# Spectra by even and odd tokens, the last modulation group in two parts, and a new order of the first stage

## What is computed

```python
mod = (cond @ w_ada[l] + b_ada[l])[:, None, :]
sh1, sc1, g1, sh2, sc2, g2 = jnp.split(mod, N_MOD, axis=-1)
h = x * (1.0 + sc1) + sh1
z = h @ w_in[l] + b_in[l]
...
k = jnp.concatenate([h_fwd.at[0].add(h_bwd[0]), jnp.zeros((1, ch), h_fwd.dtype), h_bwd[:0:-1]], axis=0)
return jnp.fft.rfft(k, axis=0)
...
y = jnp.fft.irfft(jnp.fft.rfft(uf, n=2 * L, axis=1) * k_spec[None], n=2 * L, axis=1)[:, :L]
```

## Time and profile before

| | |
|---|---|
| median of three runs | 2633.13 us (2633.02 to 2635.64) |
| profiled execution | 2630.96 us, its span 2629.6 us |
| TensorE busy | 2597.2 us (99%) |
| VectorE, ScalarE busy | 1845.6 us (70%), 1289.7 us (49%) |
| read from HBM, written | 586.24 MB, 10.49 MB |

### The profile page before, as it was taken

One profiled execution on the slowest core, in us unless ns is written; L12 is line 12 of the kernel. 1 busy time (PEld: TensorE's weight loads), 2 busy tenths in 40 slices (PEclk: granted clock), 3 DMA queues, 4 the chain that ended last, 5 costly groups with the idle time before them and its releaser, 6 DMA issues.

```text
span 2629.6 us, 31620 instructions
## 1 busy us (share of the span) xinstructions
PE 2597.2 (99%) x12546; PEld 2169.0 (82%) x12546; DVE 1845.6 (70%) x1927; ACT 1289.7 (49%) x1566; POOL 32.1 (1%) x55
## 2 busy tenths in 40 slices
PE   7999999999999999999999999999999999999999
PEld 3789988878888888888888888888888888988887
DVE  9978989988876644687776767756554665666565
ACT  2455444444444444555555544444444654545463
POOL 0000000000000000000000000000000000000000
PEclk9999999999999999999999999999999999999999
DMA  9998877798688755666555665555655556634554
GB/s 399 382 371 303 305 283 286 273 338 315 238 297 283 247 185 188 193 204 203 192 192 193 192 191 177 192 190 184 211 192 192 183 185 172 177 125 160 192 177 143
DMA packets 276584, 598.65 MB, mean 228 GB/s; under 512 B 21264, under 2 KB 46288, under 8 KB 260064
## 3 DMA queue, kind: packets, MB, share of 16 engines
q1 hardware_dynamic: 268272, 566.52, 63.2%
q0 software_dynamic: 4560, 21.56, 2.5%
q10 hardware_dynamic: 3616, 8.68, 0.8%
HBM read 586.24 MB, written 10.49 MB: 227 GB/s over the span
## 4 chain that ended last, share of the span: by engine, by line
PE 89%; DVE 7%; DMA 2%; issue 1%; ACT 1%; ACTq 0%; DVEq 0%; SPq 0%
PE ps L951 26%; PE ps L953 26%; PE ps L952 26%; DVE group_acc L2390 2%; PE ps L1076 2%; DVE w_lo L2271 2%; PE ps L1060 2%; PE ps L1063 1%; PE ps L1062 1%; DMA raw<-in_k_in 1%; PE ps L1461 1%; PE ps L1463 1%; PE ps L1462 1%; DMA raw<-in_w_in 1%; DVE ada_acc L2299 1%
## 5 line engine op out<-in xcount | busy, mean ns | idle before, releaser
L2271 DVE TENSOR_TENSOR w_lo<-raw,w_hi 128x1024 fp32r<-128x1024 f32 x870 | 1050.3, 1221 | 663.0 <-ACT w_hi L1607 661.0
L1607 ACT CAST w_hi<-raw 128x1024 fp32r<-128x1024 f32 x870 | 906.8, 1051 | 1074.5 <-PE ps L953 900.2
L951 PE MATMUL ps<-w_lo,x_hi 128*128 128x512 f32 x2592 | 1019.5, 393 | 6.6 <-DVE w_lo L2271 2.8
L953 PE MATMUL ps<-w_hi,x_lo 128*128 128x512 f32 x2592 | 1010.7, 390 | 0.0
L952 PE MATMUL ps<-w_hi,x_hi 128*128 128x512 f32 x2592 | 1010.0, 390 | 0.0
L951 PEld LDWEIGHTS ps<-w_lo,x_hi 128*128 128x128 f32 x2592 | 487.4, 188 | 111.9 <-DVE w_lo L2271 4.6
L953 PEld LDWEIGHTS ps<-w_hi,x_lo 128*128 128x128 f32 x2592 | 487.1, 188 | 102.1
L952 PEld LDWEIGHTS ps<-w_hi,x_hi 128*128 128x128 f32 x2592 | 487.6, 188 | 99.8 <-issue 1.0
L2299 DVE SCALAR_TENSOR_TENSOR ada_acc<-raw,cond,ada_acc 128x2048 f32<-128x2048 f32 x64 | 150.1, 2345 | 2.5 <-DMA raw<-in_w_ada 1.5
L951 PE MATMUL ps<-w_lo,pooled_hi 128*128 128x512 f32 x384 | 150.3, 391 | 0.0
L953 PE MATMUL ps<-w_hi,pooled_lo 128*128 128x512 f32 x384 | 149.5, 389 | 0.0
(11 more groups left out here) (379 smaller groups left out, 2135.9 us busy)
## 6 DMA issues: line engine op xcount, KB each, us to landing
raw<-in_w_m SPq DMA_DIRECT2D x128, 1024.0 KB, 5.2
raw<-in_w_ada SPq DMA_DIRECT2D x64, 1024.0 KB, 6.0
raw<-in_pool_w_in SPq DMA_DIRECT2D x64, 1024.0 KB, 5.3
raw<-in_w_in SPq DMA_DIRECT2D x56, 1024.0 KB, 7.3
raw<-in_k_mod SPq DMA_DIRECT2D x32, 1024.0 KB, 7.3
raw<-in_pool_w_out SPq DMA_DIRECT2D x32, 1024.0 KB, 5.0
raw<-in_ple_w_gate SPq DMA_DIRECT2D x32, 1024.0 KB, 5.1
raw<-in_mla_w_in SPq DMA_DIRECT2D x24, 1024.0 KB, 5.1
```

The lines of the kernel that those rows point to most:

```text
L951: mm(bank, xh, wl, start=start, stop=False)
L953: ins = mm(bank, xl, wh, start=False, stop=stop)
L1607: nc.scalar.copy(by_ktile(st, w_hi[st.half_slot(j, half)][:, 0:n]), raw_half(st, j, half)).then_inc(hi_split, 1)
L2271: tt(by_ktile(st, w_lo[slot][:, 0:n]), raw_half(st, j, half), by_ktile(st, w_hi[slot][:, 0:n].bitcast(F32)), ALU.subtract).then_inc(lo_spl ...
```

## The change

A spectrum is no longer made of all 256 tokens in one product. The transform's columns for the frequencies f and 255 - f agree on even tokens and differ in sign on odd ones (for the imaginary part the other way round), so `spectrum` now multiplies even and odd tokens apart, two matmuls in place of four, and stores both parts; the tables are cut accordingly (`dft_f`, `dft_i`). The sum and the difference are formed when a spectrum is used, by `filter_low` and `filter_high` on VectorE in `in_g`. The fourth modulation group is loaded as two groups of two k-tiles (3 and 4), four loads each, added in four operations of 128x512 for each load. The weights of group 3 are laid out so that a load holds two k-tiles of two chunks (`last_half`). ScalarE makes the first scaled piece of groups 0 to 3 (`group_first`). All four lists have a new order; the stores of spectra 0 and 1 stand after the last cast of `in_vu`, those of 2 and 3 at hooks 10 and 11 of `in_h`, and the small column loads at the beginning. Of the diff, the orders in the middle of the first stage on TensorE, ScalarE and VectorE are left out.

```diff
 W2 = [("ww", "ww")] * 2
 STREAM = [
-    ("first", 1, [("ggggggggwggg", ""), ("wgggggggggwg", ""), ("wggwggwwgwgw", ""), ("ggwwgggwwww", "")]),
+    ("first", 1, [("gggggggggggg", ""), ("gwggwgggwggw", ""), ("gwgggwwggwgw", ""), ("gwwgwggwwgw", "")]),
     ("in_vu", 1, [("w", "aa")]), ("in_h", 2, A2), ("in_h2", 1, [("wwa", "wwaa")] * 2), ("in_g", 4, [("wwaa", "wwaa"), ("ww", "ww")]),
     ("mix", 1, [("ww", "a")] * 8), ("w_o", 1, [("ww", "wawa")] * 4),
...
 
-FIRST_W = [(0, 0), (0, 1), (0, 2), (1, 1), (1, 0), (1, 2), (0, 3), (2, 1),
-           (2, 0), (1, 3), (2, 2), (2, 3), (3, 0), (3, 2), (3, 1)]
+FIRST_W = [(0, 0), (1, 1), (0, 2), (0, 1), (1, 0), (1, 2), (1, 3), (0, 3),
+           (2, 2), (2, 3), (2, 1), (2, 0), (3, 0), (3, 1), (3, 2)]
+CHUNK_FIRST, PART_LAST = [(0, 0), (0, 2), (1, 1), (1, 3)], (2, 3)
 
 
...
+        return (ST["first"], group_weights(3, n)) if n < 3 else (ST["in_vu"], 0)
+
+    def last_done(c):
+        stage, j = last_unit(2 + c // 2)
+        return stage.half(0, j) + c % 2 + 1
...
+        pieces(0, 0, 4)
         sync.dma_start(w3[:], a["k_w3"]).then_inc(w3_in, 16)
+        sync.dma_start(dft_f[:].rearrange("p m t n -> p (m t n)"), a["k_dft_f"]).then_inc(dft_in, 16)
+        pieces(0, 4, 5)
         load_window(0)
-        pieces(0, 3, 4)
-        sync.dma_start(dft[:, 0:2].rearrange("p m t n -> p (m t n)"), a["k_dft"][0]).then_inc(dft_in, 16)
-        pieces(0, 4, 8)
-        weights(0, 0)
-        load_window(1)
+        pieces(0, 5, 8)
         pieces(1, 0, 3)
         load_x(0)
+        load_window(1)
+        pieces(1, 3, 5)
+        weights(0, 0)
+        pieces(1, 5, 7)
+        weights(1, 1)
+        pieces(1, 7, 8)
+        load_bias(0, IN_COLS[0])
+        load_x(1)
+        pieces(2, 0, 2)
+        load_x(2)
+        weights(0, 2)
+        pieces(2, 2, 4)
         weights(0, 1)
-        pieces(1, 3, 4)
+        pieces(2, 4, 5)
+        weights(1, 0)
+        pieces(2, 5, 8)
+        weights(1, 2)
+        weights(1, 3)
+        pieces(3, 0, 2)
+        weights(0, 3)
+        load_bias(2, IN_COLS[2])
+        pieces(3, 2, 3)
+        weights(2, 2)
+        pieces(3, 3, 4)
+        weights(2, 3)
+        load_bias(3, IN_COLS[3])
+        weights(2, 1)
+        pieces(4, 0, 1)
+        weights(2, 0)
+        pieces(4, 1, 3)
+        weights(3, 0)
+        load_x(3)
+        weights(3, 1)
         load_bias(1, IN_COLS[1])
-        pieces(1, 4, 8)
-        pieces(2, 0, 4)
-        weights(0, 2)
-        load_x(1)
-        pieces(2, 4, 5)
-        weights(1, 1)
-        load_x(2)
-        pieces(2, 5, 7)
-        weights(1, 0)
-        pieces(2, 7, 8)
-        pieces(3, 0, 1)
-        weights(1, 2)
-        weights(0, 3)
-        pieces(3, 1, 2)
-        load_x(3)
-        weights(2, 1)
-        pieces(3, 2, 3)
-        weights(2, 0)
-        pieces(3, 3, 5)
-        weights(1, 3)
-        weights(2, 2)
-        pieces(3, 5, 8)
-        weights(2, 3)
-        weights(3, 0)
+        pieces(4, 3, 4)
         weights(3, 2)
-        load_bias(2, IN_COLS[2])
-        load_bias(3, IN_COLS[3])
-        weights(3, 1)
         load(ST["in_vu"], 0, 0, a["k_in"][3, 3])
-        load_bias(0, IN_COLS[0])
...
             pe.wait_ge(filt_win, 2 * it + m + 1)
-            for f in range(2):
-                for t in range(2):
-                    ins = mm(ps[:, spec_bank(it, m) + f, :], dft[:, m, t, f * P:(f + 1) * P],
-                             (h_sum, h_dif)[m][:, t, :], start=t == 0, stop=t == 1)
+            for t in range(2):
+                ins = mm(ps[:, spec_bank(it, m) + (1 - t if m else t), :], dft_f[:, m, t, :], (h_sum, h_dif)[m][:, t, :],
+                         start=True, stop=True)
             ins.then_inc(spec_mm, 1)
 
         def group_sum(q):
-            pe.wait_ge(group_added, 8 * (q + 1))
-            for n in range(8):
+            pe.wait_ge(group_added, 15 * (q + 1) + q // 4)
+            for n in range(8 if q < 3 else 4):
                 ins = mm(ps[:, sum_bank(q), n:n + 1], group_acc[q % 2][:, n * P:(n + 1) * P], ones[:, 0:1],
                          start=True, stop=True)
             ins.then_inc(group_summed, 1)
 
         st = ST["first"]
 
-        def group_half(q, c, half, first=None, last=None):
+        def group_half(q, c, half):
             pe.wait_ge(fm_lo if half else h_lo, q + 1)
             products(st, 0, group_weights(q, c), half, 4 * q + 2 * half, x_hi, x_lo, pair(c),
-                     q == 0 and half == 0 if first is None else first, q == 3 and half == 1 if last is None else last)
...
+            group_half(q, c, 1)
+
+        def last_half(n, half):
+            c, part = 2 * (n % 2) + half, n // 2
+            pe.wait_ge(fm_lo if part else h_lo, 4)
+            stage, j = last_unit(n)
+            products(stage, 0, j, half, 12 + 2 * part, x_hi, x_lo, pair(c), c == 3 and part == 0, part == 1)
...
+        group_unit(1, 3)
+        group_unit(0, 3)
         group_unit(2, 2)
+        group_unit(2, 3)
+        group_half(2, 1, 0)
         pe.wait_ge(part_kept, 1)
         group_sum(3)
+        group_half(2, 1, 1)
+        group_unit(2, 0)
+        last_half(0, 0)
+        last_half(0, 1)
+        last_half(1, 0)
         pe.wait_ge(mod_group, 4)
-        group_unit(2, 3, True, False)
-        group_unit(3, 0)
-        group_unit(3, 2)
...
+        def group_first(q):
+
+            st, j = ST["first"], group_ada(q, 0)
+            act.wait_ge(raw_full[st.slot(j)], st.landed(0, j))
+            if q == 0:
+                act.wait_ge(cond_ready, 1)
+            elif q >= 2:
+                act.wait_ge(group_summed, q - 1)
+            n = 2 * CH if q < 3 else CH
+            nc.scalar.activation(group_acc[q % 2][:, 0:n], raw[st.slot(j)][:, 0:n], ACT.Copy, scale=cond[:, 0:1]) \
+                .then_inc(group_begun, 1)
...
+        group_first(0)
...
+            act.wait_ge(mod_group, 5 if q + half == 4 else q + 1)
...
+        columns_load()
+        group_first(1)
         spectrum_out(0, 0)
-        group_round(0, 0)
         spectrum_out(0, 1)
         group_hi(0, 0)
+        spectrum_out(1, 0)
+        group_round_half(0, 0, 0)
...
-        act.wait_ge(half_used, first_half(1, 3, 1))
+        group_round_half(2, 0, 0)
+        act.wait_ge(half_used, first_half(*PART_LAST, 1))
         nc.scalar.copy(part_u[:], ps[:, 6:8, :]).then_inc(part_kept, 1)
-        group_round(2, 3)
-        spectrum_store(0)
-        group_round(3, 0)
+        group_round_half(2, 0, 1)
+        group_round_half(3, 0, 0)
         group_hi(3, 0)
-        group_round_half(3, 2, 0)
+        group_round_half(3, 0, 1)
+        group_round(3, 1)
+        group_round(3, 2)
         group_hi(3, 1)
-        group_round_half(3, 2, 1)
-        group_round(3, 1)
-        spectrum_store(1)
         round_half(ST["in_vu"], 0, 0, 0)
         round_half(ST["in_vu"], 0, 0, 1)
+        spectrum_store(0)
+        spectrum_store(1)
...
+        def in_h_10():
+            round_dft(0)
             gelu(3)
-            sgu_std(0, 0)
-
-        run_at(st, 0, {0: lambda: gelu(0), 3: lambda: spectrum_store(2), 7: lambda: columns_load(), 8: in_h_8, 12: lambda: sgu_std(0, 1)})
+            spectrum_store(2)
+
+        run_at(st, 0, {3: lambda: gelu(0), 5: lambda: gelu(1), 9: lambda: gelu(2), 10: in_h_10, 11: lambda: spectrum_store(3), 12: lambda: sgu_std(0, 1)})
...
+            parts = 2 if q < 3 else 4
+            k, n = parts * u + e, 4 * CH // parts
+            if k > 1 or q == 4 and k:
+                dve.wait_ge(group_added, 15 * q + k - (q < 4))
+            elif k:
+                dve.wait_ge(group_begun, q + 1)
+            else:
+                dve.wait_ge(group_summed, q - 1)
+            buf = group_acc[q % 2][:, 0:n]
+            part = raw[st.slot(j)][:, e * n:(e + 1) * n]
+            gain = cond[:, k:k + 1]
+            if k == 0:
+                ins = tsc(buf, part, gain, None, ALU.mult)
+            else:
+                ins = stt(out=buf, in0=part, scalar=gain, in1=buf, op0=ALU.mult, op1=ALU.add)
+            ins.then_inc(group_added, 1)
+
         def add_first(q, u):
 
...
+        group_rest_half(2, 2, 1)
         add_first(3, 3)
-        add_first(3, 4)
-        group_rest(1, 3)
-        group_rest(2, 2)
-        for u in range(5, 8):
-            add_first(3, u)
-        group_rest_half(2, 3, 0)
+        group_rest(2, 3)
+        add_part(4, 0, 0)
+        group_rest(2, 1)
+        add_part(4, 0, 1)
+        add_part(4, 0, 2)
+        add_part(4, 0, 3)
+        group_rest(2, 0)
+        add_first(4, 1)
         group_scale(3)
-        group_rest_half(2, 3, 1)
-        group_rest(3, 0)
+        add_part(4, 2, 0)
+        add_part(4, 2, 1)
+        add_part(4, 2, 2)
+        group_rest_half(3, 0, 0)
         group_lo(3, 0)
+        add_part(4, 2, 3)
+        group_rest_half(3, 0, 1)
+        group_rest_half(3, 1, 0)
+        add_part(4, 3, 0)
+        group_rest_half(3, 1, 1)
+        add_part(4, 3, 1)
+        add_part(4, 3, 2)
+        add_part(4, 3, 3)
```

(20 more changed lines are left out.)

278 lines of the change are left out of this document (142 added, 136 removed).

## The result

The changed kernel takes 2651.11 us (median; 2646.77 to 2652.88), the kernel before 2633.15 beside it: a ratio of 1.0065, 95% interval 1.0053 to 1.0077. It is 18 us slower where 1 us was forecast, and lies outside the range. The profiled execution is 2651.37 us, its span 2650.0, so against that of before (2630.96) the traces have 20.4 us to explain; the profiled run of before was 2.2 us faster than its median.

What follows compares the result with a forecast made beforehand. Transfers, VectorE and TensorE were taken as nearly full at once in the first stage. 7.0 - 1.3 - 2.0 - 4.5 = -0.8, and 0.2 for smaller waits, made 1.0 us slower: 2634 us, range 2625 to 2641.

Steps and rivals of the forecast that it cites:

- What bounds the kernel: First stage, before in_h: transfers, VectorE and TensorE nearly full at once; what counts is which ends last.
- the prediction's second step: Apparently Part 2: the first stage's new order, placed by counting bytes, with a gain of 7.0 us.
- Part 1: Spectra by even and odd tokens in the first stage: 10.8 us less TensorE work, 0.6 us less transfer.
- Rival (c): First stage: saved matmuls don't show, TensorE not being the limit before 60 us; contained in the forecast, no own chance.
- Part 2: New order of the first stage: last narrow add near 143, in_h begins at 158.7; gain 7.0 us, bounds 1 and 10.
- Rival (b): First stage: VectorE becomes the bound, last add after 147 us, gain only 1.0; 7 us slower, 2640; chance 0.20.
- Part 3: First scaled piece on ScalarE: VectorE about even, nothing taken; range -1.5 to +1.5 us.
- Part 4, start of `in_h`: Store 1 lands about where in_h would begin and vu_out(2) waits for it: 1.3 us lost, bounds 0 and 3.
- Part 4, thirteenth half: In in_h, conv_center(0) waits for stores 2 and 3, delaying the rest: 2.0 us lost, bounds 0 and 4.
- Lower clock: A clock drop behind the new stall, outside the sum, would cost up to 1.7 us more.
- Part 5: Two filter operations more on VectorE in each in_g round: 4.5 us lost, bounds 2.5 and 6.
- the 0.6 of slack: Deduction in in_g from the filter operations' 5.1 us sum, leaving 4.5 us lost.

Runs made afterwards that it cites:

- x6: Kernel before, its orders unchanged, with the spectra by even and odd tokens and the filter operations: 2639.03 us (1.002).
- x9: Changed kernel with all but the first two additions of each modulation group cut to 8 columns, every transfer kept: 2641.86 us (1.0043).
- x1: Changed kernel without the two filter operations of each in_g round: 2641.26 us (1.0028).
- x7: Changed kernel with the filter sums formed on GpSimd behind each spectrum's load instead of on VectorE: 2653.74 us (1.0089).
- x11: Changed kernel, stores 2 and 3 at in_h halves 3 and 5, vu_out(1) and vu_out(2) at its first half, last group scaled earlier: 2645.7 us.
- x4: Changed kernel with vu_out(1) and vu_out(2) ahead of the rests of in_h's first load: 2647.44 us (1.0056).
- x14: Changed kernel with stores 2 and 3 at halves 3 and 5 of in_h and store 0 at half 7: 2644.56 us (1.0045).
- x3: Changed kernel with stores 2 and 3 at hooks 3 and 5 of in_h instead of 10 and 11: 2644.37 us (1.0039).
- x10: Changed kernel with the three edits of x11 and the filter sums on GpSimd: 2650.45 us (1.0074).
- x16: Changed kernel with all mends of order as in x15, but the filter operations of in_g left out: 2638.88 us (1.002).
- x13: Changed kernel with the last spectrum copied out of PSUM before the two casts of weights (1,2) on ScalarE: 2645.45 us (1.0048).
- x15: Changed kernel with the edits of x11, x13 and x14 together, filter operations kept in in_g: 2644.42 us (1.0043).
- x12: Changed kernel with the three edits of x11 and the filter operations of in_g left out: 2639.39 us (1.0021).
- x5: Changed kernel with the old spectra of four matmuls and no filter operations, the new orders alone: 2640.81 us (1.0027).

## Why the prediction was wrong, point by point

**What bounds the kernel.** Right: three resources were nearly full. It followed that little is won when one is relieved, and the prediction's second step forgot it.

**Part 1.** Spectrum records fell to 32 in all, but after the first product 21 are left (10.7 us), not 16 (7.2):

```profile
L1140 PE MATMUL ps<-h_dif,dft_f 128*128 128x512 f32 x12 | 5.8, 608 | 0.5 <-DVE h_dif L2408 0.5
L1140 PE MATMUL ps<-h_sum,dft_f 128*128 128x512 f32 x9 | 4.9, 656 | 1.6 <-DVE h_sum L2408 1.6
```

Against the earlier trace rows 7.3 us of TensorE are saved, not 10.8, and x6 shows what the split is worth in the old order: 0.7 us. Rival (c) was treated as contained in the forecast; it was the main fact of this part.

**Part 2, the step that failed first.** Forecast gain 7.0, measured 1.1. The first product was right (near 49; 49.7). The last narrow add was put at 143 and ended at 148.7. The step counted the bytes ahead of the last piece and divided them by the rates of the earlier trace rows, on the ground that these rates contain the waits of the slots. The count was right: the piece landed at 144.5 with 54.8 MB moved, for 54.5 said. The rate failed: by 140 us 1.2 MB less had been moved, 3.3 us at 373 GB/s. Another 1.1 us came from a rest of VectorE between the four adds. A rate is a result of the order it was read in. What lowered it is not settled. That VectorE freed the slots later is not shown: it was less busy than before, and from 20 to 150 us SyncE waited 109.6 us for slots, where it had waited 107.0. Rival (b) gave the criterion (last add after 147) and its price (gain 1.0), and both came true. Of its cause, VectorE and transfers in series, x9 shows only that VectorE's additions are worth 3.3 us in the new order. The swing of -1.8 to +3.0 us between kernels with nearly the same first stage was not in the range; of its cause the runs show only that x1, x7 and x11, the three late ones, had 6.8 to 10.2 us of lower clock behind 99 us, at waits of 3.2 to 3.5 us for the last spectrum's copy, where the changed kernel had 3.4 at a wait of 2.2.

**Part 3.** Even, as said: scalings and additions of VectorE are 80.7 us against 80.0.

**Part 4, start of `in_h`.** Forecast a loss of 1.3 (at most 3), measured a wait of 5.6 and 2.1 of clock. Store 1 landed at 164.4, where the first stage ended, as said. The step asked only when store 1 lands for the semaphore of `vu_out(2)`. It did not ask what the two stores do to the load that is on the way beside them, nor what stands ahead of `vu_out(1)` and `vu_out(2)` on VectorE: two rests of that very load. x4 put `vu_out` ahead of the rests and won 2.9 us of the wait, x14 took one store away and won 1.3 more than x3. Why the load took 12.7 us here and 5.9 and 6.5 in x9 and x10, beside the same two stores, is open.

**Part 4, thirteenth half.** Forecast 2.0, bounds 0 and 4; by the prediction's own measure it was 4.0: the half began 40.8 us after `in_h` did, where 38.8 was said and 36.8 had been. The path was the one named: store pair, `conv_center(0)`, side taps, rest, and TensorE waited the 3 to 4 us that were to show it. Mis-sized was the pair. Store 2 went out at 189.95 as expected, but its packets began 2.3 us later, not 1.0, and the two took 10.2 us, not 8.2. The rule cited there (Trainium skill, DMA: Bandwidth & Descriptors, Queues, rings and completion order: the queues are served in turn) would have made them 8.9. From 192 to 202.8 us the stores' queue q10 had 47.1% of the engines' time beside 37.4% for q1 and 14.4% for a third queue, q0, which the forecast didn't count; in turn or not, that is no equal share. From the start of `in_h` to its fourteenth half x3 loses 0.7 us where the changed kernel loses 6.2.

**Lower clock.** It stood outside the sum, as up to 1.7 us. At the two new waits it cost 2.1 and 2.2, at 335 us 1.6 more: 5.9 us, as much as part 2 was wrong by. The 1.6 is not the filter operations' doing: x16 has none and the same 6.8 us of lower clock in that round.

**Part 5.** Forecast 4.5 (bounds 2.5 and 6), measured 7.7, and 7.2 by x1. First round at nothing: right. Two things make the rest, and VectorE's second round shows both. It begins at 367.71 in the kernel before and at 380.16 in the changed one:

```profile
381.92 4.80 DVE L2299 SCALAR_TENSOR_TENSOR ada_acc<-raw,cond,ada_acc 128x2048 f32<-128x2048 f32 x2
386.64 1.22 DVE L2638 TENSOR_TENSOR hy_lo<-ps,hy_hi 128x1024 fp32r<-128x1024 f32 x1
...
399.36 1.22 DVE L2613 TENSOR_TENSOR prod_re<-hy_re,spec 128x1024 f32<-128x1024 f32 x1
```

```profile
395.41 2.35 DVE L2344 SCALAR_TENSOR_TENSOR ada_acc<-raw,cond,ada_acc 128x2048 f32<-128x2048 f32 x1 [0.96 <-DMA raw<-in_w_ada]
398.56 2.35 DVE L2344 SCALAR_TENSOR_TENSOR ada_acc<-raw,cond,ada_acc 128x2048 f32<-128x2048 f32 x1 [0.79 <-DMA raw<-in_w_ada]
400.83 1.22 DVE L2729 TENSOR_TENSOR hy_lo<-ps,hy_hi 128x1024 fp32r<-128x1024 f32 x1
...
414.58 1.22 DVE L2704 TENSOR_TENSOR prod_re<-hy_re,spec 128x1024 f32<-128x1024 f32 x1
```

From `hy_lo` to `prod_re`, where the filter operations stand, VectorE takes 13.75 us instead of 12.72. In the three rounds this stretch is 1.0, 1.6 and 2.2 us longer, 4.9 in all (4.9 to 5.3 in x3, x6, x13 and x15), for 1.3, 1.7 and 2.1 said: the idle pieces of the earlier trace rows did cover what was credited to them. Only the 0.6 of slack was not there. What the step left out stands ahead of `hy_lo`. The additions of the modulation (`ada_acc`) wait for their loads, and `hy_lo` comes 1.7, 1.0 and 0.2 us later in its round than before, 2.9 in all. Beside the filter operations such a delay is paid in full; in x1, without them, `hy_lo` comes 1.1 us later in the third round, and the round loses only 0.5. Why these loads come later than in the kernel before is open; in x3 and x15 the one of the second round is absent.

**Rivals and chances.** (b) was right on the first stage and had 0.20; but its sum of 7 us slower took the losses behind the stage as in the forecast, and 18 were measured. No case held a longer start of `in_h` or a clock that answers each wait, which is why the range ended ten microseconds too low.

What the runs settle, in medians above the kernel before: the filter operations cost 5.5 to 6.3 us with the stores mended (x12 against x11, x16 against x15) and 11 without (x1 against the changed kernel). The place of stores 2 and 3 costs 7.9 with the filter operations in (x3). Without them it can't cost as much: x1 and x5 have the stores where the changed kernel has them and are at 7.0 and 6.6, x12 and x16 have them moved and are at 5.0 and 5.9. So these prices hold beside each other only in part, and must not be added up. Some 5 us stay with the new order whatever was moved. Open are why it moves fewer bytes, and which piece of it does that: the order of the loads, the last group in two parts and the first pieces on ScalarE were never run apart. No kernel here beats the one before.
